# Attention's transposed probabilities: one two-bank PSUM tensor, or three of one bank filled in pieces

## The reference

```python
logits = jnp.einsum('bqhd,bqkhd->bqkh', qb, k_sel) * scale + bias
logits = jnp.where(valid[..., None], logits, NEG_INF)
probs = jax.nn.softmax(logits, axis=2)
return jnp.einsum('bqkh,bqkhd->bqhd', probs, v_sel)
```

## Time and profile before

| | before |
|---|---|
| median of 3 runs | 1870.96 us |
| the profiled execution's own time | 1869.98 us |
| its span in the trace | 1868.2 us |
| attention, from the first logits matmul to the last output copy | 493.19 to 634.47 us, 141.28 us |
| one middle pair of heads, from logits of tile 6 to the next logits of tile 6 | 535.91 to 568.62 us, 32.71 us |

### The profile page before, as it was taken

The page is one execution under the profiler, slowest core; times in us unless marked ns, Lnnn a source line. Parts: engine busy times, 40 slices in busy tenths (PEclk is TensorE's granted clock), DMA queues, the critical chain, the costliest instruction groups (busy, mean ns, idle before and its releaser), DMA issues.

```text
span 1868.2 us, 34085 instructions
## 1 busy us (share of the span) xinstructions
PE 1710.1 (92%) x14120; PEld 1371.1 (73%) x14120; DVE 1151.4 (62%) x2145; ACT 764.9 (41%) x1207; POOL 318.3 (17%) x291
## 2 busy tenths in 40 slices
PE   8978999999688688897599999999999999999896
PEld 7735777778455478786478788888888888888685
DVE  3479899989588347676337565544446644444755
ACT  4264745565466433332244333322333322223541
POOL 1101233322133101222122110000021000001322
PEclk9998999999799889998599999999999999999998
DMA  4101134543110321300353332323332333233222
GB/s 137 35 3 42 47 116 118 158 160 113 47 46 25 150 86 49 94 13 14 124 189 102 100 92 91 102 91 101 94 98 91 120 106 101 91 101 94 78 77 90
DMA packets 87432, 167.53 MB, mean 90 GB/s; under 512 B 7216, under 2 KB 47824, under 8 KB 87280
## 3 DMA queue, kind: packets, MB, share of 16 engines
q1 hardware_dynamic: 86704, 164.32, 27.5%
q10 hardware_dynamic: 576, 1.05, 0.2%
HBM read 136.51 MB, written 28.84 MB: 89 GB/s over the span
## 4 chain that ended last, share of the span: by engine, by line
PE 48%; DVE 1%; ACT 1%; POOL 1%; DMA 0%; issue 0%; POOLq 0%; SPq 0%; ACTq 0%; DVEq 0%
PE acc L602 16%; PE acc L603 16%; PE acc L604 16%; DVE y L336 0%; DVE x L734 0%; DMA rows_raw<-y_rwkv 0%; PE post_spread L331 0%; POOL pre_squares_total L297 0%; DVE w_lo L670 0%; PE post_means L310 0%; POOL post_squares_total L297 0%; PE pre_spread L331 0%; PE pre_means L310 0%; ACT w_hi L506 0%; ACT ffn_hi_lo L567 0%
## 5 line engine op out<-in xcount | busy, mean ns | idle before, releaser
L602 PE MATMUL acc<-h_hi,w_hi 128*128 128x512 f32 x768 | 304.6, 397 | 21.8 <-DVE w_lo L670 15.8
L603 PE MATMUL acc<-h_lo,w_hi 128*128 128x512 f32 x768 | 300.8, 392 | 0.0
L604 PE MATMUL acc<-h_hi,w_lo 128*128 128x512 f32 x768 | 300.7, 392 | 0.0
L506 ACT ACTIVATE w_hi<-w_raw 128x1024 fp32r<-128x1024 f32 x160 | 168.4, 1053 | 142.6 <-DMA w_raw<-w_ffn 142.6
L670 DVE TENSOR_TENSOR w_lo<-w_raw,w_hi 128x1024 fp32r<-128x1024 f32 x160 | 206.5, 1292 | 7.5 <-ACT w_hi L506 7.5
L602 PE MATMUL acc<-ffn_hi_lo,w_hi 128*128 128x512 f32 x512 | 200.3, 391 | 1.3 <-DVE ffn_hi_lo L718 1.3
L604 PE MATMUL acc<-ffn_hi_lo,w_lo 128*128 128x512 f32 x512 | 199.2, 389 | 0.0
L603 PE MATMUL acc<-ffn_hi_lo,w_hi 128*128 128x512 f32 x512 | 199.2, 389 | 0.0
L602 PEld LDWEIGHTS acc<-h_hi,w_hi 128*128 128x128 f32 x768 | 145.1, 189 | 54.7 <-DVE w_lo L670 16.5
L297 POOL TENSOR_TENSOR post_squares_total<-post_squares_total,post_squares 128x512 f32<-128x512 f32 x40 | 57.3, 1433 | 693.5 <-ACT post_squares L290 692.0
L237 PE MATMUL z_acc<-h_hi,w_in_hi 128*128 128x512 f32 x416 | 165.8, 399 | 8.4 <-PEq L1827 8.4
(11 more groups left out here) (301 smaller groups left out, 3439.5 us busy)
## 6 DMA issues: line engine op xcount, KB each, us to landing
w_raw<-w_ffn SPq DMA_DIRECT2D x128, 512.0 KB, 3.5
w_in_raw<-w_in SPq DMA_DIRECT2D x31, 512.0 KB, 3.6
rwkv_factors<-rs_then_masks_and_values SPq DMA_DIRECT2D x28, 512.0 KB, 6.4
factors<-rwkv_factors SPq DMA_DIRECT2D x32, 448.0 KB, 6.8
w_raw<-w_out SPq DMA_DIRECT2D x16, 512.0 KB, 3.6
w_raw<-w_gate SPq DMA_DIRECT2D x16, 512.0 KB, 3.5
rs_then_masks_and_values<-xT SPq DMA_DIRECT2D x16, 256.0 KB, 6.3
x<-xT SPq DMA_DIRECT2D x16, 256.0 KB, 4.0
```

Source lines behind the costliest of these rows:

```text
L506: act.activation(wh[:, g % RING, :], w_raw[:, g % RING, :], ACT.Copy).then_inc(rounded, 1)
L602: pe.matmul(out, w_hi, a_hi, start=first, stop=False)
L603: pe.matmul(out, w_hi, a_lo, start=False, stop=False)
L604: return pe.matmul(out, w_lo, a_hi, start=False, stop=last)
```

## The change

The tensor `ps_probs_transposed` of two banks becomes three tensors of one bank. The turns of all steps are cut into pieces of at most 4 blocks (512 columns), numbered through the whole stage; piece n goes to tensor n % 3. A piece waits for the copy of piece n-3, and its last transpose raises `turned`. ScalarE copies piece by piece. Tiles of 5 to 8 blocks give two pieces for each head, tiles of 1 to 4 blocks one: 96 pieces in place of 64 turns. The bank for this comes from the outputs: `ps_o` is one tensor with two places of 128 columns in one bank, and weigh(k) waits for copy_y(k-1), where it waited for copy_y(k-2).

```diff
-        ps_p = ctx.pb("ps_probs_transposed", [P, SEQ], F32)
-        ps_o = [ctx.pb(f"ps_o{v}", [P, HALF], F32) for v in range(2)]
+        ps_p = [ctx.pb(f"ps_probs_transposed{v}", [P, HALF], F32) for v in range(3)]
+        ps_o = ctx.pb("ps_o", [P, 2, P], F32)
...
+        def pieces(k, e):
+
+            before = sum(2 * (tile(x)[1] * P // HALF + 1) for x in range(k)) + e * (tile(k)[1] * P // HALF + 1)
+            keys = (tile(k)[1] + 1) * P
+            return [(before + n, slice(c, min(c + HALF, keys))) for n, c in enumerate(range(0, keys, HALF))]
+
+        def pieces_to(k, e):
+            return pieces(k, e)[-1][0] + 1
...
                 pe.wait_ge(divided, 2 * k + e + 1)
-                if k >= 1 or e == 1:
-                    pe.wait_ge(turned_copied, 2 * k + e)
-                for b in range(t + 1):
-                    last = pe.transpose(ps_p[:, b * P:(b + 1) * P], pr[k % (AHEAD + 1)][e][:, b * P:(b + 1) * P], ident[:, :])
-                last.then_inc(turned, 1)
+                for n, cut in pieces(k, e):
+                    need(pe, turned_copied, n - 2)
+                    for at in range(cut.start, cut.stop, P):
+                        last = pe.transpose(ps_p[n % 3][:, at - cut.start:at - cut.start + P], pr[k % (AHEAD + 1)][e][:, at:at + P], ident[:, :])
+                    last.then_inc(turned, 1)
...
-                pe.wait_ge(turned_copied, 2 * k + 2)
-                if k >= 2:
-                    pe.wait_ge(done, k - 1)
+                pe.wait_ge(turned_copied, pieces_to(k, 1))
+                need(pe, done, k)
...
-                        last = pe.matmul(ps_o[k % 2][f, 0:P], va[:, b, p, f], ptr[k % 2][e][:, b * P:(b + 1) * P], start=(b == 0), stop=(b == t))
+                        last = pe.matmul(ps_o[f, k % 2, :], va[:, b, p, f], ptr[k % 2][e][:, b * P:(b + 1) * P], start=(b == 0), stop=(b == t))
...
-                act.wait_ge(turned, 2 * k + e + 1)
                 if k >= 2:
                     act.wait_ge(weighted, k - 1)
-                act.activation(ptr[k % 2][e][:, 0:(t + 1) * P], ps_p[:, 0:(t + 1) * P], ACT.Copy).then_inc(turned_copied, 1)
+                for n, cut in pieces(k, e):
+                    act.wait_ge(turned, n + 1)
+                    act.activation(ptr[k % 2][e][:, cut], ps_p[n % 3][:, 0:cut.stop - cut.start], ACT.Copy).then_inc(turned_copied, 1)
...
-                dve.tensor_copy(yo[p % 2][:, t * P:(t + 1) * P], ps_o[k % 2][:, 0:P]).then_inc(done, 1)
+                dve.tensor_copy(yo[p % 2][:, t * P:(t + 1) * P], ps_o[:, k % 2, :]).then_inc(done, 1)
...
-                    dve.wait_ge(turned, 2 * (k - AHEAD - 1) + e + 1)
+                    dve.wait_ge(turned, pieces_to(k - AHEAD - 1, e))
```

## The result

The changed kernel takes 1857.30 us in the median of 8 runs (1855.18 to 1860.57); before takes 1868.39 in the median of its 8 (the three known at the forecast have their median at 1870.96). The medians lie 11.1 us apart; the ratio of the fast runs is 0.9947, 95% interval 0.9932 to 0.9962, which is 9.9 us, 7 to 13. In a second set of runs the ratio was 0.9957 (0.9941 to 0.9973).

A forecast was written before the change was run, and what follows sets the result against it. TensorE was taken to bound attention. Four pairs at 1.07 us give 4.3, the start 0.7, the end 1.1 and 0.1: 6.2 saved, so 1863.8, plus 0.98 for the median: 1864.8 us, range 1858.5 to 1871.5.

The forecast's parts named there:

- The recorded sign of being wrong: In attention, an 8-block turn was to hold TensorE about 1.16 us; if as long as before, time nearer 1861.
- What comes on TensorE: Tiles of 5 to 8 blocks get 8 more pieces a pair, each boundary 0.13 us: 1.04 a pair, 4.2 in all.
- Both ends of the bound: Price of TensorE's added piece boundaries: nothing from below, 0.20 us each from above by the loads, 6.4 in all.
- The rival of the free boundary: A piece boundary costs TensorE nothing, so 4.2 us more are gained: 1860.6 us; chance 0.16.
- What goes: TensorE's waits for ScalarE's copies in a middle pair all go with three banks: 2.22 us a pair.
- What the new wait costs: weigh(k-1) waits for copy_y(k-2) on VectorE: 0.1 us at weigh(10) and 0.08 at weigh(14) in a pair.
- the cover that I counted for weigh(8): At weigh(8), starting 0.53 us earlier, its output copy was to end at about 541.71, in time.
- The rival of the added wait: weigh held by the output copy at every step: 1.73 us a pair, 6.9 in all, 1871.7 us; chance 0.09.
- VectorE takes the bound: TensorE's freed time becomes waits for scalings and row maxima; only start and end give, 1869.4 us; chance 0.15.
- What comes on ScalarE: 96 copies taking about 46.4 us, 5.1 more ScalarE work, 1.3 a pair; exponentials behind the copies not late.
- A slip in the sum: Gain at logits(11) put at -0.11 us: one boundary each in turn(8, 0) and turn(8, 1), less the 0.19 wait.

The follow-up runs named there:

- runs 5 to 7: Changed kernel plus, in turn: satisfied waits ahead of transposes; a semaphore increment at each transpose; waits on two semaphores. One execution each: 1858.02, 1862.11, 1868.29 us.
- runs 2 to 4: Changed kernel with two piece banks and old outputs; with two piece banks; with the output copy between the two scalings: 1859.53, 1861.75, 1858.20 us.
- run 5: Changed kernel with 183 more already satisfied waits, ahead of every transpose but the first of its piece: 1858.02 us in one execution.
- Runs 7 and 9: Changed kernel with two satisfied waits ahead of transposes; changed kernel with output copy between scalings and divide(15) ahead of row_max(16): 1868.29 us (one execution), 1860.79 us.

## Why the prediction was wrong

The direction and the place were right, and so was what the wait was for. The forecast is 7.5 us above the measured median. Of these, 2.6 are the base (1870.96 by three runs, 1868.39 by eight), 1.8 are attention (6.2 forecast, 8.0 measured), and the last 3.1 are what the medians show beyond attention (1.9 by the ratio). The interval of the total is 2.8 us to each side, so those are not shown to be an effect of the change. So with the base right the time would have been inside the range.

That attention came within 1.8 us was partly luck, since its errors cancelled. In a pair the boundaries gave 1.04 us more than forecast and the waits that went 0.39 more, while 1.00 more came back in new waits: 1.51 in place of 1.07. The recorded sign of being wrong, "if a turn of 8 takes as long as before, and then the time is nearer to 1861", is what came. By its steps:

- **"What comes on TensorE", a boundary at 0.13 us: failed.** It costs nothing that shows (1.02 for a turn of 8 before and after; runs 5 to 7). That was 1.04 us a pair and 4.2 in all, the largest mis-sized term. I had read a change of group, from transposes to matmuls, as a boundary of pieces. Both ends of the bound were written down, and the lower one held. The rival of the free boundary, given 0.16, was right in its mechanism. Its time, 1860.6, kept the other terms of the forecast and so had 10.4 us for attention where 8.0 were measured; that it lies nearer to 1857.30 is no support for its sum.
- **"What goes", 2.22 us a pair: too small.** From start to next start before and after, the groups in front of freed turns and logits shrank by 2.61: the idle time that the timeline names begins at a modelled end. weigh(9) lost 0.80, not 0.73. The turns behind ScalarE's small copies had waited 0.07 with no idle time shown at all, as turn(9, 1) at 544.39, 0.14 after the end of turn(9, 0)'s copy at 544.25. The 0.26 in front of turn(11, 0) did not go: the turn now waits 0.28 for its scaling.
- **"What the new wait costs", 0.18 a pair: too small.** It is 0.54 to 0.57 by runs 2 to 4. I took it as biting at weigh(10) and weigh(14); it bites at four weighs. With the boundaries free TensorE came to each of them earlier, so the cover that I counted for weigh(8) was gone: copy_y(7), the row below, ends at 572.69 and weigh(8) starts at 572.84. The rival of the added wait put it at 1.73 if it bit everywhere.
- **"VectorE takes the bound", given 0.15: partly.** From start to start logits(17), which wait for row maxima, come 0.15 later (the wait shown grew from 0.41 to 0.53), and logits(13) 0.10 later, again behind row maxima. All increases in a pair are 1.10 where I had 0.1: 0.66 at the four weighs, these 0.25, and 0.19 in steps of 0.04 or less whose cause is not shown. 2.61 - 1.10 is 1.51.
- **"What comes on ScalarE": right.** 96 copies take 46.0 us by shape, 46.4 was forecast. Of a pair's 16 exponentials the first two start 0.06 and 0.07 us later in the pair than before, each of the others 0.55 to 1.78 earlier.
- **A slip in the sum.** Two boundaries of 0.13 less the 0.19 give -0.07 at logits(11), not -0.11; it changes nothing of the above. Measured, logits(11) start 0.23 earlier in the pair.

VectorE's copy_y(7) in the changed kernel:

```profile
572.41 0.28 DVE L2051 COPY y_out<-ps_o 128x128 f32<-128x128 f32 x1
```

The copies of the changed kernel by shape, against the earlier trace rows (count, busy us, mean ns):

```profile
L2019 ACT ACTIVATE probs_transposed<-ps_probs_transposed 128x512 f32<-128x512 f32 x48 | 27.7, 597 | 23.1 <-PE ps_probs_transposed L1983 23.1
...
L2019 ACT ACTIVATE probs_transposed<-ps_probs_transposed 128x384 f32<-128x384 f32 x16 | 7.8, 487 | 3.7 <-PE ps_probs_transposed L1983 3.7
...
L2019 ACT ACTIVATE probs_transposed<-ps_probs_transposed 128x256 f32<-128x256 f32 x16 | 6.1, 379 | 4.4 <-PE ps_probs_transposed L1983 4.4
...
L2019 ACT ACTIVATE probs_transposed<-ps_probs_transposed 128x128 f32<-128x128 f32 x16 | 4.4, 275 | 2.3 <-PE ps_probs_transposed L1983 2.3
```

By thirds of the stage, the second profile of the changed kernel against the first of before: the first pair and its start 42.72 to 40.60 (2.1, forecast 1.8), two middle pairs 65.41 to 62.42 (3.0, forecast 2.1), the end 31.72 to 28.68 (3.0, forecast 2.3). Each third missed on the same side. The first depends on when the clock rises; run 5, where it rises about as late as in before's first profile, gives 40.65 there.

The range was too narrow at its lower end because it took in the free boundary with the rest of the sum unchanged, and nothing for the base, a median of three runs that lay 7.9 us apart.

## What to carry to other kernels

When a producer waits for the whole of a long copy, cut both into pieces first, over the buffers that are there: here that gave all of the gain (32.71 to 30.67 us a pair), and the extra bank nothing, while what was given up for it cost 0.54. Price a boundary by a boundary of the same kind; one read where the kind of work changes gave 0.13 us here for something that costs nothing. A wait that another wait covers is free only as long as that one stays, so price it again with the other gone, and measure groups from start to next start, since modelled ends hid gaps of up to 0.2 us here.

## What the runs showed of the hardware

With 183 more satisfied waits, 192 more increments, or waits on two semaphores ahead of every transpose, a turn of 8 blocks still held TensorE for 1.02 us. And the granted clock may fall in a stage that has it at full speed in another execution. In the first profile of the changed kernel, one us for each row (columns as in the earlier trace rows):

```profile
530.00:531.00 1.00, 0.49 (x4) 0.33 (x4) 1.00 (x4) 1.00 (x3) 0.65 (x1) 1.00 0.00 0
531.00:532.00 1.00, 0.26 (x2) 0.27 (x3) 0.96 (x5) 1.00 (x3) 0.07 (x1) 1.00 0.08 16
...
533.00:534.00 1.00, 1.00 (x14) 1.00 (x12) 0.96 (x3) 0.38 (x1) 0.97 (x2) 0.50 0.00 0
534.00:535.00 1.00, 1.00 (x9) 0.67 (x6) 1.00 (x2) 0.00 (x0) 0.00 (x0) 0.50 0.00 0
```

TensorE was busy for 0.49 and 0.26 us of these two before its clock fell, at 532.40, to 0.50, 1.2 GHz, and from there to the next logits 3.37 us went by (532.42 to 535.79) where the next pair took 1.83 (565.16 to 566.99). The same holes are in the next pair, at 1.00. Runs 7 and 9 have such a stretch of 3.4 us at about the same place of the first pair (from 533.44 and from 534.75), the second profile of the changed kernel has none. What makes the difference is not shown.
